# TensorE transpositions as ordinary fp32 matmuls with the identity, in a two-block, one-core transformer kernel

## The chip, the core and the metric

The kernel runs on one core of one Trainium2 chip. The metric is the device time of one execution in microseconds; the median of three runs before the change is 1362.98 us (1362.72 to 1365.19). TensorE (PE) does the matmuls, VectorE (DVE) and ScalarE (ACT) the elementwise work, and GpSimd (POOL) and SyncE (SP) start transfers.

## The reference, cut to what matters

Two blocks of two layers each work on 256 tokens of width 1024, all in fp32. Every layer is a normalisation, a mixer, a residual add, a normalisation and a squared-ReLU MLP:

```python
for layer in range(DEPTH):                      # first block
    u = rms_norm(h, mix_norm_g[layer])
    h = h + even_mixer(u, ...)                  # layer 0: 8 heads of top-k attention, 8 of compressed/selected/window attention
    # layer 1: h = h + diff_mixer(u, ...)       # 8 heads, each the difference of two softmaxes
    h = h + sq_relu_mlp(rms_norm(h, mlp_norm_g[layer]), mlp_w_up[layer], mlp_w_down[layer])
# second block: layer 0 pools over trailing windows, layer 1 is attention of 16 heads with a position bias;
# norms are followed by a scale and shift, residual adds by a gate
```

Transpositions are no part of the mathematics. They are there because a matmul contracts over partitions: the normalised activations, each head's softmax and the attention's output lie with tokens on partitions and are wanted with channels (or keys) on partitions.

## The kernel before

Weights come as a stream of 179 pieces of 1 MB into a ring of four. ACT copies each piece to a rounded form `whi` (L323), DVE makes the remainder `wlo` (L522), and PE forms each product in three passes of the rounded type (helper `three`, L1047). The activations are split likewise into `uh` and `ul`. Almost all of the time is this stream: four MLPs of 32 pieces, three mixers with projections of 10 to 12 pieces in front and 4 behind, and one pooling piece. The order of each engine's work is written out by hand, and semaphores tie the engines together.

PE transposes in these places:

- `norm(e)` (L1105), eight times (e = 0, 1, 2, 3, 5, 6, 7, 8). DVE writes the scaled activations `ut` in quarters (L557), PE turns 16 blocks of 128x128 into four PSUM banks, and after each pair of blocks of the second token half it signals ACT. ACT writes `uh` (L345), or in the second block `work` or `qk` (L349), DVE the rest (L571, or L579 and L580), and the next projection or MLP starts with piece k as soon as `ul` of block k is there.
- `turn` (L1172), once for each head's softmax `P`: 24 heads in layer 0 (phase e), 8 in layer 1 (phase d), 16 in the last attention (phase b). It turns three blocks of 128x128 into bank 3. DVE copies the bank to `PT` (L650), and `values` (L1179 to L1181) multiplies it with the values. PE's order in phases e and b is, per head: scores (L1158) and masks (L1161) of head i, values of head i-3, turn of head i-2. In phase d one turn comes for two scores.
- `turn_out` (L1190), once for each of the three attentions: 16 blocks of the output `o_` into banks 0 to 3, ACT and DVE split them (L385, L655), and `project` (through `add_rows`, L1047) follows.
- two small places (L1259 and L1317), which the change leaves as they are.

`ident` is the fp32 identity in `con`. In layer 0, `hidden` (L1252) is run between the first four heads, and the compressed branch (L1268, L1270, L1280, L1317, L1322) between later ones. DVE and ACT also split four weight pieces between those heads. `spread_col` (L1112) is an ordinary fp32 matmul of a broadcast column with `ident`, 128 columns wide; `swapped` and `dswap` (L1210, L1333) are ordinary fp32 matmuls of 512 columns.

Of the kernel before, what the change touches and what calls it, by code (L numbers as in the profile page):

```python
# [51 lines left out]
TURN = (2, 3, 4, 5)  # L52
# [14 lines left out]
def build(nc, a):  # L67
# [3 lines left out]
    with ctx:  # L71
# [48 lines left out]
        bank = [ctx.enter_context(nc.psum_tensor(f"bank{i}", [128, 512], fp32)) for i in range(8)]  # L120
# [3 lines left out]
        ident = con[:, C_ID:C_ID + 128]  # L124
# [7 lines left out]
        o_ = vo[:, 1, :, :]  # L132
# [4 lines left out]
        ut = uf.rearrange("p (t n) -> p t n", t=NT)  # L137
# [73 lines left out]
        def u_no(e):  # L211

            return 8 * (e if e < 4 else e - 1)
# [20 lines left out]
        def even_map(i):  # L234
            kind, h = i // 8, i % 8
            if kind == 0:
                return QA + h // 2, 64 * (h % 2), KA, tk, slice(0, 64), (4, 5)
            g, j = h // 4, h % 4
            vs = 128 * (kind - 1) + 64 * g
            return QB + j, 64 * g, (KS, KW)[kind - 1], v_, slice(vs, vs + 64), ((6, 7), (4, 5))[kind - 1]  # L240
# [798 lines left out]
        def _(pe):  # L1039
            mm = nc.tensor.matmul  # L1040

            def three(out, w_first, wh, wl, xh, xl, start, stop):

                for i, (wa, xa) in enumerate(((wh, xh), (wh, xl), (wl, xh)) if w_first else
                                             ((wh, xh), (wl, xh), (wh, xl))):
                    st, mv = (wa, xa) if w_first else (xa, wa)
                    ins = mm(out, st, mv, start=start and i == 0, stop=stop and i == 2, skip_group_check=True)  # L1047
                return ins
# [5 lines left out]
            def features(m, out, sems=None, blocks=2):  # L1054

                wh, wl = weights(m)
                for k in range(KB):
                    if sems is not None:
                        s, base, per = sems
                        pe.wait_ge(s, base + k // per + 1)  # L1060
                    for b in range(blocks):
                        c = slice(128 * b, 128 * b + 128)
                        ins = three(out[:, 256 * b:256 * b + 256], True, wh[:, k, c], wl[:, k, c], uh[:, k, :], ul[:, k, :],
                                    k == 0 and b == 0, k == KB - 1)
                return ins

            def tokens(m, out, c0, n, o0=0, width=None, w=None):
                wh, wl = weights(m) if w is None else w
                for t in range(NT):
                    for k in range(KB):  # L1070
                        ts = slice(128 * t, 128 * t + 128)
                        ins = three(out[:, o0 + n * t:o0 + n * t + n], False, wh[:, k, c0:c0 + n], wl[:, k, c0:c0 + n],
                                    uh[:, k, ts], ul[:, k, ts], t == 0 and k == 0 and o0 == 0, k == KB - 1)
                return ins
# [24 lines left out]
            def norm(e):  # L1099
                for t in range(NT):  # L1100
                    for q in range(4):
                        pe.wait_ge(u_ready, u_no(e) + 4 * t + q + 1)
                        for b in (2 * q, 2 * q + 1):
                            c = 256 * (b % 2) + 128 * t
                            ins = nc.tensor.transpose(bank[TURN[q]][:, c:c + 128], ut[:, t, 128 * b:128 * b + 128], ident)  # L1105
                        if t:
                            ins.then_inc(turned, 1)

# [58 lines left out]
            def turn(ph, i, src):  # L1167

                if i >= 1:
                    pe.wait_ge(s_pt[ph], i)  # L1170
                for c in range(3):
                    ins = nc.tensor.transpose(bank[3][:, 128 * c:128 * c + 128], src[:, 128 * c:128 * c + 128], ident)  # L1172
                ins.then_inc(s_tr[ph], 1)

            def values(ph, i, vv, vs, dst):
# [7 lines left out]
            def turn_out(r, after):  # L1183

                pe.wait_ge(o_ready, after)
                for j in range(4):
                    for b in (2 * j, 2 * j + 1):
                        for t in range(NT):
                            c = 256 * (b % 2) + 128 * t
                            ins = nc.tensor.transpose(bank[j][:, c:c + 128], o_[:, t, 128 * b:128 * b + 128], ident)  # L1190
                    ins.then_inc(oT_ready, 1)

            def project(m0, r, e):
# [4 lines left out]

            pe.wait_ge(in_con, 16)
            norm(0)  # L1200

            order = [0, 1, 3, 4, 5, 6, 7, 8, 9]
# [9 lines left out]
            for i in range(10):  # L1212
                pe.wait_ge(lo_ready, i + 1)
                if i == 2:
# [3 lines left out]
                    ins = tokens(i, bank[0], 0, 92, w=w)  # L1218
                elif i in (8, 9):
                    pe.wait_ge(e_t2, order.index(i - 2) + 1)  # L1220
                    features(i, bank[i % 2], blocks=1)
                    ins = tokens(i, bank[i % 2], 128, 128, o0=256)
                else:
# [6 lines left out]
                    ins = features(i, bank[i % 2], (ul_ready, 0, 1) if i == 0 else None)  # L1230
# [56 lines left out]
            for i in range(24 + 3):  # L1287
                if i < 24:
                    q, r0, k, vv, vs, ob = even_map(i)
# [9 lines left out]
                if i >= 3:  # L1299
                    j = i - 3  # L1300
                    q, r0, k, vv, vs, ob = even_map(j)
# [6 lines left out]
                if 2 <= i < 26:  # L1308
                    pe.wait_ge(s_exp["e"], i - 1)
                    turn("e", i - 2, P[:, (i - 2) % 4, :])  # L1310
# [8 lines left out]
                if i == 23:  # L1319
                    pe.wait_ge(o_free, 2)  # L1320
                    for t in range(NT):
                        ins = mm(bank[6 + t][:, :], pcT[0:CW, t, :], vbd[0:CW, :, :], start=True, stop=True)  # L1322
                    ins.then_inc(oc_ps, 1)
            turn_out(0, NT)
            project(MLP0 - 4, 0, 1)
            norm(1)
            mlp(0)
            pe.wait_ge(spread_out, 2)
            norm(2)

            def dswap(i):
# [15 lines left out]
            for i in range(8 + 2):  # L1347
                if i < 8:
                    for c in range(2):
                        scores("d", 2 * i + c, i, 8 + i, 64 * c, causal)  # L1350
                if i >= 2:
                    j = i - 2
                    hs = slice(128 * (j % 4), 128 * (j % 4) + 128)
                    values("d", j, v_, slice(128 * j, 128 * j + 128), [bank[4 + j // 4][:, hs], bank[6 + j // 4][:, hs]])
                if 1 <= i < 9:
                    pe.wait_ge(s_cmb, i)
                    turn("d", i - 1, P[:, 2 * (i - 1) % 4, :])
            turn_out(1, 2 * NT)
            project(MLP1 - 4, 1, 3)
            norm(3)  # L1360
# [8 lines left out]
            for g in range(4):  # L1369
                pe.wait_ge(p_h, g + 1)  # L1370
                for t in range(NT):
                    ts = slice(128 * t, 128 * t + 128)
                    for k in range(2):
                        ins = three(bank[4 + 2 * t + g // 2][:, 256 * (g % 2):256 * (g % 2) + 256], False,
                                    wp[0][:, g, k, :], wp[1][:, g, k, :], uh[:, 2 * g + k, ts], ul[:, 2 * g + k, ts],
                                    g % 2 == 0 and k == 0, g % 2 == 1 and k == 1)
# [21 lines left out]
            for i in range(16 + 3):  # L1398
                if i < 16:
                    pe.wait_ge(h_in[i % 8], 16 * (i // 8 + 1))  # L1400
                    scores("b", i, i // 2, 8 + i // 2, 64 * (i % 2),
                           [(slice(0, 128), flip, hank[:, i % 8, 128:256]), (slice(128, 384), flip, hank[:, i % 8, :])])
                if i >= 3:
                    j = i - 3
                    hs = slice(64 * (j % 8), 64 * (j % 8) + 64)
                    values("b", j, v_, slice(64 * j, 64 * j + 64), [bank[4 + j // 8][:, hs], bank[6 + j // 8][:, hs]])
                if 2 <= i < 18:
                    pe.wait_ge(s_exp["b"], i - 1)
                    turn("b", i - 2, P[:, (i - 2) % 4, :])
            turn_out(2, 3 * NT)  # L1410
            project(MLP3 - 4, 2, 8)
            norm(8)
# [116 lines left out]
```

## Time and profile before

| | |
|---|---|
| median of 3 runs | 1362.98 us |
| the profiled execution's own time | 1365.05 us |
| its span, first to last instruction | 1363.3 us |
| PE busy | 1254.2 us (92%) |
| DVE / ACT busy | 839.5 us (62%) / 546.9 us (40%) |
| mean granted clock of PE | 0.926 |

Between the span and the execution's own time lie 1.75 us. In the trace, a matmul's duration contains a tail in which the next one already runs, so the pace of a run of matmuls is read from their starts, or from a merged row as (its length minus one instruction's length) over (count minus one). The granted clock has two levels here, 1.0 (2.4 GHz) and 0.5 (1.2 GHz). Names such as `bank<-con,P` are the tiles that an instruction writes and reads.

### The profile page before, as it was taken

What the parts mean: (1) busy time and instruction counts of PE and PEld (TensorE: products, weight loads), DVE (VectorE), ACT (ScalarE), POOL (GpSimd) and SP (SyncE); (2) the same over time, 40 slices, a digit from 0 to 9 for tenths busy, and PEclk for the clock granted to TensorE, in tenths of its full rate; (3) what the DMA queues carried; (4) which work ended last, traced back from release to release, by engine and by line L of the source; (5) the groups of instructions that cost most, each with busy time, mean ns of one, the idle gap of its engine ahead of it and who ended that gap; (6) DMA issues with size and microseconds to landing.
All of it is one profiled execution on the core that took longest, in us unless ns stands there. A gap on an engine that the chain in (4) does not pass through costs nothing.

```text
span 1363.3 us, 18272 instructions
## 1 busy us (share of the span) xinstructions
PE 1254.2 (92%) x7662; PEld 1100.6 (81%) x7662; DVE 839.5 (62%) x1168; ACT 546.9 (40%) x754; POOL 44.1 (3%) x86
## 2 busy tenths in 40 slices
PE   5989898899998998699999939999979998899997
PEld 4975676799997986579999838999969877799996
DVE  5662543677777664657777787777773444755554
ACT  5302232544444324344444455444444442544442
POOL 1010000000000000000000000000001010000000
PEclk9998557899999997799999969999989998999999
DMA  8413110587876343057787715777735520455540
GB/s 301 153 47 124 62 62 12 183 290 283 282 281 243 125 155 124 1 201 278 279 280 281 250 64 207 280 281 283 283 138 197 195 72 32 141 183 188 187 150 32
DMA packets 35074, 245.72 MB, mean 180 GB/s; under 512 B 4272, under 2 KB 4304, under 8 KB 6064
## 3 DMA queue, kind: packets, MB, share of 16 engines
q1 hardware_dynamic: 26352, 189.13, 39.3%
q0 software_dynamic: 8496, 54.43, 11.2%
q8 instruction: 61, 1.00, 0.3%
q10 hardware_dynamic: 144, 0.98, 0.2%
q14 instruction: 21, 0.17, 0.0%
HBM read 242.93 MB, written 1.07 MB: 179 GB/s over the span
## 4 chain that ended last, share of the span: by engine, by line
PE 83%; DVE 10%; ACT 4%; issue 2%; DMA 1%; SPq 0%; DVEq 0%; ACTq 0%
PE bank L1047 67%; PE bank L1158 4%; DVE wlo L522 2%; ACT whi L323 2%; PE bank L1172 2%; PE bank L1161 2%; PE bank L1105 1%; PE bank L1252 1%; PE bank L1179 1%; PE bank L1181 1%; PE bank L1180 1%; DMA raw<-in_stream 1%; PE bank L1190 1%; DVE x L538 1%; DVE work L536 1%
## 5 line engine op out<-in xcount | busy, mean ns | idle before, releaser
L522 DVE TENSOR_TENSOR wlo<-raw,whi 128x2048 fp32r<-128x2048 f32 x175 | 399.4, 2283 | 289.8 <-ACT whi L323 289.8
L323 ACT ACTIVATE whi<-raw 128x2048 fp32r<-128x2048 f32 x175 | 333.8, 1909 | 252.9 <-PE bank L1047 251.9
L1047 PE MATMUL bank<-uh,whi 128*128 128x256 f32 x1408 | 406.7, 289 | 4.5 <-DVE ul L571 3.6
L1047 PE MATMUL bank<-ul,whi 128*128 128x256 f32 x1408 | 400.5, 284 | 0.0
L1047 PE MATMUL bank<-uh,wlo 128*128 128x256 f32 x1408 | 400.1, 284 | 0.0
L1047 PEld LDWEIGHTS bank<-uh,whi 128*128 128x128 f32 x1408 | 272.4, 193 | 13.0 <-issue 7.5
L1047 PEld LDWEIGHTS bank<-ul,whi 128*128 128x128 f32 x1408 | 272.4, 193 | 5.1 <-issue 2.9
L1047 PEld LDWEIGHTS bank<-uh,wlo 128*128 128x128 f32 x1408 | 272.1, 193 | 0.0
L1047 PE MATMUL bank<-whi,hh 128*128 128x512 f32 x512 | 200.4, 391 | 2.4 <-DVE hl L597 2.2
L1047 PE MATMUL bank<-wlo,hh 128*128 128x512 f32 x512 | 199.9, 390 | 0.0
L1047 PE MATMUL bank<-whi,hl 128*128 128x512 f32 x512 | 199.2, 389 | 0.0
L359 ACT ACTIVATE work<-bank 128x512 f32<-128x512 f32 x64 | 38.3, 598 | 227.2 <-PE bank L1047 227.2
L1047 PEld LDWEIGHTS bank<-whi,hh 128*128 128x128 f32 x512 | 96.3, 188 | 22.4 <-DVE wlo L522 2.7
L604 DVE CUSTOM_DVE_ANT_0 qk<-qk,cb 128x1024 f32<-128x1024 f32 x96 | 113.4, 1218 | 0.0
L1047 PEld LDWEIGHTS bank<-whi,hl 128*128 128x128 f32 x512 | 96.1, 188 | 20.6
L1047 PEld LDWEIGHTS bank<-wlo,hh 128*128 128x128 f32 x512 | 96.3, 188 | 17.5
L1047 PE MATMUL bank<-whi,uh 128*128 128x512 f32 (+3 forms) x224 | 83.3, 372 | 9.3 <-DVE ul L990 9.3
L377 ACT ACTIVATE P<-bank,nmax 128x128 f32<-128x128 f32 x56 | 20.6, 367 | 154.4 <-DVE nmax L643 154.4
L1047 PE MATMUL bank<-wlo,uh 128*128 128x512 f32 (+3 forms) x224 | 81.5, 364 | 0.0
L1047 PE MATMUL bank<-whi,ul 128*128 128x512 f32 (+3 forms) x224 | 81.3, 363 | 0.0
L1158 PE MATMUL bank<-qk 64*128 64x128 f32 x224 | 68.9, 442 | 5.8 <-ACT P L379 2.1
L1105 PE MATMUL bank<-con,u 128*128 128x128 f32 x128 | 28.0, 407 | 48.8 <-DVE u L557 48.8
(204 smaller groups left out, 1149.2 us busy)
## 6 DMA issues: line engine op xcount, KB each, us to landing
raw<-in_stream SPq DMA_DIRECT2D x178, 1024.0 KB, 4.9
qk<-in_w_mod POOLq DMA_DIRECT2D x48, 1024.0 KB, 5.2
u<-bias_rows POOLq DMA_DIRECT2D x16, 128.0 KB, 4.6
x<-in_x SPq DMA_DIRECT2D x2, 512.0 KB, 8.6
vo<-in_fin_g POOLq DMA_DIRECT2D x2, 512.0 KB, 6.4
out_y<-vo SPq DMA_DIRECT2D x2, 512.0 KB, 2.6
con<-in_con ACTq DMA_DIRECT2D x1, 955.5 KB, 7.4
raw<-in_stream SPq DMA_DIRECT2D x1, 368.0 KB, 14.8
```

The lines of the kernel that those rows point to most:

```text
L323: nc.scalar.activation(whi[:, c % RING, 0:w], raw[:, n % RING, 0:w], ACT.Copy).then_inc(hi_ready, 1)
L359: nc.scalar.activation(work[:, s % 2, :], bank[s % 2][:, :], ACT.Relu).then_inc(relu_done, 1)
L377: nc.scalar.activation(P[:, i % size, 0:128], b[:, 0:128], ACT.Exp, bias=nmax[:, i, 0:1], accum_out=sums[:, i, 0:1])
L522: nc.vector.tensor_tensor(wlo[:, c % RING, 0:w], raw[:, raw_index(c) % RING, 0:w], whi[:, c % RING, 0:w].bitcast(fp32), ALU.subtract).then ...
L536: link(nc.vector.tensor_tensor(work[:, i, :], bank[4 + 2 * t + h][:, :], gate[:, 512 * h:512 * h + 512], ALU.mult))
L538: nc.vector.tensor_tensor(xs, work[:, i, :], xs, ALU.add).then_inc(x_ready, 1)
L604: ins = nc.vector.tensor_tensor_reduce(out=stage[j][:, r, :], in0=stage[j][:, r, :], in1=cb[:, :], scale=1.0, scalar=0.0, op0=ALU.mult, op ...
L1047: ins = mm(out, st, mv, start=start and i == 0, stop=stop and i == 2, skip_group_check=True)
L1105: ins = nc.tensor.transpose(bank[TURN[q]][:, c:c + 128], ut[:, t, 128 * b:128 * b + 128], ident)
L1158: mm(b[:, c0:c1], qk[rows_, q, 128 * t:128 * t + 128], qk[rows_, k, 0:c1 - c0], start=t == 0, stop=False, skip_group_check=True)
L1161: ins = mm(b[:, dst], st, mv, start=False, stop=n == len(masks) - 1, skip_group_check=True)
L1172: ins = nc.tensor.transpose(bank[3][:, 128 * c:128 * c + 128], src[:, 128 * c:128 * c + 128], ident)
```

## The change

Three calls are replaced; operands, destinations, order and semaphores stay:

```diff
@@ norm (L1105) @@
-                            ins = nc.tensor.transpose(bank[TURN[q]][:, c:c + 128], ut[:, t, 128 * b:128 * b + 128], ident)
+                            ins = mm(bank[TURN[q]][:, c:c + 128], ut[:, t, 128 * b:128 * b + 128], ident, start=True, stop=True)
@@ turn (L1172) @@
-                    ins = nc.tensor.transpose(bank[3][:, 128 * c:128 * c + 128], src[:, 128 * c:128 * c + 128], ident)
+                    ins = mm(bank[3][:, 128 * c:128 * c + 128], src[:, 128 * c:128 * c + 128], ident, start=True, stop=True)
@@ turn_out (L1190) @@
-                            ins = nc.tensor.transpose(bank[j][:, c:c + 128], o_[:, t, 128 * b:128 * b + 128], ident)
+                            ins = mm(bank[j][:, c:c + 128], o_[:, t, 128 * b:128 * b + 128], ident, start=True, stop=True)
```

Both forms load the block as the stationary operand and move the identity past it. The old form is PE's transpose mode, the new one a plain fp32 product. The transpositions of L1259 and L1317 keep the old form.

## Rows read from the trace of the kernel before

**Rows 1.** The page: busy time and share of each engine; slices, granted clock.

```profile
PE 1254.2 (92%) x7662; PEld 1100.6 (81%) x7662; DVE 839.5 (62%) x1168; ACT 546.9 (40%) x754; POOL 44.1 (3%) x86
...
PEclk9998557899999997799999969999989998999999
```

**Rows 2.** The page: the chain that ended last, shares of the span by line.

```profile
PE bank L1047 67%; PE bank L1158 4%; DVE wlo L522 2%; ACT whi L323 2%; PE bank L1172 2%; PE bank L1161 2%; PE bank L1105 1%; PE bank L1252 1%; PE bank L1179 1%; PE bank L1181 1%; PE bank L1180 1%; DMA raw<-in_stream 1%; PE bank L1190 1%; DVE x L538 1%; DVE work L536 1%
```

**Rows 3.** Groups by form, TensorE: count | busy, mean ns | idle before.

```profile
L1172 PE MATMUL bank<-con,P 128*128 128x128 f32 x144 | 31.8, 343 | 1.6 <-DVE P L925 1.1 <-ACT P L379 0.4
L1105 PE MATMUL bank<-con,u 128*128 128x128 f32 x128 | 28.0, 407 | 48.8 <-DVE u L557 48.8
...
L1190 PE MATMUL bank<-con,vo 128*128 128x128 f32 x48 | 10.8, 418 | 14.9 <-DVE vo L957 8.4 <-DVE vo L856 3.5 <-DVE vo L1020 3.0
```

**Rows 4.** Timeline, TensorE: start, us, engine, line, operation, form, count (full, full, half, half).

```profile
829.44 1.95 PE L1112 MATMUL bank<-con,mod 128*128 128x128 f32 x16
...
214.27 0.50 PE L1172 MATMUL bank<-con,P 128*128 128x128 f32 x3
...
179.21 0.85 PE L1172 MATMUL bank<-con,P 128*128 128x128 f32 x3
...
251.80 3.68 PE L1105 MATMUL bank<-con,u 128*128 128x128 f32 x16 [3.79 <-DVE u L557]
```

**Rows 5.** The chain in order of time: swaps at half, at full clock.

```profile
39.38 1.76 PE bank L1210 x2
...
466.72 0.86 PE bank L1333 x2
```

**Rows 6.** Stretches: length, busy PE, PEld, DVE, ACT, POOL (instructions), granted clock, DMA.

```profile
571.70:575.00 3.30, 3.19 (x15) 3.19 (x16) 1.27 (x3) 1.71 (x3) 0.00 (x0) 0.50 0.00 0
575.20:578.60 3.40, 3.40 (x17) 2.83 (x16) 1.59 (x3) 0.85 (x2) 0.00 (x0) 1.00 0.00 0
...
164.60:210.40 45.80, 45.72 (x180) 34.27 (x181) 20.88 (x46) 14.57 (x50) 0.00 (x0) 0.50 0.16 60
1094.00:1128.00 34.00, 33.57 (x214) 26.37 (x215) 15.90 (x42) 13.30 (x60) 3.22 (x6) 1.00 0.24 59
...
527.40:544.30 16.90, 14.70 (x54) 9.71 (x53) 10.03 (x31) 7.23 (x33) 0.00 (x0) 0.50 0.18 62
544.50:561.30 16.80, 14.53 (x95) 10.08 (x93) 12.63 (x42) 6.88 (x32) 0.00 (x0) 1.00 0.01 1
```

**Rows 7.** The same for line 1172 alone (turns): PE, PEld, PEclk.

```profile
128.00:213.30 85.30, 16.11 (x57) 12.48 (x57) 0.50 0.14 50
526.00:544.50 18.50, 2.38 (x9) 1.82 (x9) 0.54 0.18 66
```

**Rows 8.** Timeline of layer 0's heads: scores of two in turn, then values.

```profile
176.16 1.65 PE L1158 MATMUL bank<-qk 64*128 64x128 f32 x4
...
179.99 1.65 PE L1158 MATMUL bank<-qk 64*128 64x128 f32 x4
...
181.75 0.64 PE L1179 MATMUL bank<-vo,PT 128*128 128x64 f32 x2
```

**Rows 9.** Timeline: the weight remainder on DVE that covers the turn at 159.47.

```profile
159.51 2.29 DVE L522 TENSOR_TENSOR wlo<-raw,whi 128x2048 fp32r<-128x2048 f32 x1 [2.32 <-ACT whi L323]
```

**Rows 10.** Timeline of norm 1: after its transpositions, and the clock's return.

```profile
255.73 0.55 PE L1047 MATMUL bank<-uh,whi 128*128 128x256 f32 x1 [0.26 <-DVE ul L571]
...
257.79 0.28 PE L1047 MATMUL bank<-uh,whi 128*128 128x256 f32 x1
```

**Rows 11.** Timeline: norm 0's follower, norm 3's transpositions, norm 5's evacuations.

```profile
19.20 0.55 PE L1047 MATMUL bank<-uh,whi 128*128 128x256 f32 x1 [2.29 <-DVE ul L571]
...
599.72 2.48 PE L1105 MATMUL bank<-con,u 128*128 128x128 f32 x16 [2.51 <-DVE u L557]
...
794.33 3.76 ACT L349 ACTIVATE qk<-bank,mod,gain 128x256 f32<-128x256 f32 x8 [2.32 <-PE bank L1105]
```

**Rows 12.** Timeline: the second turn-out.

```profile
571.81 3.61 PE L1190 MATMUL bank<-con,vo 128*128 128x128 f32 x16 [8.44 <-DVE vo L957]
```

## The prediction

> **What bounds the kernel now.** I read first the busy times [rows 1], then the chain that ended last [rows 2]. PE is busy 92% of the span and its lines carry nearly all of the chain, 67% of it in the split products (L1047). So PE is the bound almost everywhere, and what it gets more to do goes into the time unless it waited there anyway. The two largest transposing lines stand in that chain themselves, L1172 with 2% and L1105 with 1%, and L1190 with 1%. The second thing to see is the clock by slices [rows 1]: it is at half in the fifth and sixth slice, which are layer 0's attention, and dips around each normalisation. The stretches say it exactly: twelve heads of layer 0, 164.6 to 210.4, ran at 0.5 with PE busy 45.72 of 45.80 us, while the last attention, 1094 to 1128, ran at 1.0 [rows 6]. The price of the edit must therefore be taken at each of the two levels.
>
> **How many.** 144 turns of a block (48 heads of three), 128 blocks in the eight norms, 48 in the three turn-outs [rows 3]: 320 blocks, all 128x128 fp32. Each is one matmul record now.
>
> **The price of one.** The new form is in the trace already: `spread_col` moves the same identity past a stationary fp32 block of 128 columns. Its 8 products are 16 records in 1.95 us [rows 4]; with about 0.28 for the last one that is (1.95 - 0.28)/15 = 0.111 us a record and 0.223 a product. A transposition at full clock: three in 0.50 us, (0.50 - 0.28)/2 = 0.11 each [rows 4]. So a block costs one record more, 0.113 us at full clock rounded up. At half clock the old form takes (3.68 - 0.42)/15 = 0.217, and three take 0.85 [rows 4]. The new form has no row there at this shape; the nearest is a 512-column product, 1.76 us for two at half against 0.86 at full clock [rows 5], so it doubles, and a block costs 0.213 more at half clock. The bounds: nothing, if the second record hid under the load of its weights (at full clock the sixteen of spread_col show that it doesn't), and 0.45, if the old form were free. I take the row of the same form.
>
> The Trainium skill (TensorE: Matmul & The Clock Gate, Terms) calls the transpose mode four times faster for fp32, and FP8 and Floating Point Precision (TensorE Precision Notes) gives true fp32 four passes. By that the ordinary form would cost four times 0.11; the rows show twice, and the measurement decides.
>
> **Layer 0's turns (24).** 57 records of L1172, 19 turns, lie in 128 to 213.3 at half clock [rows 7]. A head there repeats every 3.83 us (179.99 - 176.16) with PE hardly idle [rows 6, 8]: scores and masks, values from 181.75, the turn behind them. Three blocks add 3 x 0.213 = 0.64, so a head takes 4.47. DVE has 20.88 us of work in those twelve heads, 1.74 each, and covers nothing. One turn, at 159.47, is covered: its copy waits for a weight remainder of 2.29 us on DVE, which ends at 161.8 [rows 9], some 1.5 us after the turn; without that cover it would be another 0.64. 18 x 0.64 = 11.5. The other 5 turns run at full clock, 3 x 0.113 = 0.34 each, on the way to the GELU and at the end: 1.7. Together 13.2.
>
> **Layer 1's turns (8).** Three at half clock [rows 7], 1.9, and five at full, 1.7: 3.6. Here the clock came back by itself within the attention, at about 544.4 [rows 6]. More PE work before that can bring it earlier; the five groups after cost PE less time than those before, and one group earlier is worth about 2.7 us (half of a group of 5.8 us less a wait or two). Between 3.6 and 0.9 I take 2.2.
>
> **The last attention's turns (16).** All at full clock, PE busy 33.57 of 34.00 [rows 6]: 16 x 0.34 = 5.4. The last few wait for copies in a chain with PE, where the price is exposed as well.
>
> **The norms (8).** After five of them (1, 2, 6, 7, 8) the picture is that of norm 1: 16 transpositions at half clock, 0.26 us of waiting, and products at half clock from 255.73, until at about 257.7 the clock is back; a product of 256 columns lasts 0.55 at 255.73 and 0.28 at 257.79 [rows 4, 10]. The old blocks and the products behind them share that half-clock time, and the new blocks take the products' place in it. If the clock comes back at the same moment, the extra work ends up at full clock: 16 x 0.113 = 1.8, less the waiting of 0.26 and a little more where it was longer, so 1.4 each, 7.0 for five. Bounds: 0.5 each (the clock earlier) and 16 x 0.213 = 3.4 (later). Norm 3 ran at full clock, paced by DVE's quarters: 2.48 us for 16 [rows 11]. Sixteen new ones take 16 x 0.223 + 0.1 = 3.7, 1.2 more, but the evacuations that the next product needs are released pair by pair before the last block, so +0.4, bounds 0 and 1.2. Norm 5 feeds the pooling through ACT, 3.76 us for eight evacuations [rows 11], which start after the tenth block and then run beside PE: +0.7, bounds 0.3 and 3.4. Norm 0 is followed by 2.29 us of waiting for the first weights [rows 11], and by products at half clock, 0.55 us for the first: of +3.4 all but about 1 is hidden, and an earlier clock would give about as much back. I take 0, bounds -1 and +1. Sum 8.1.
>
> **The turn-outs (3).** Each is 16 blocks at half clock, 3.6 us [rows 12], with the projection right behind it. By the same reasoning as for the norms 1.8 each less a wait, 4.7 together; bounds 3 and 10.
>
> **What moves besides.** Nothing in order or semaphores. ACT's and DVE's copies start later where PE does, as counted. The ring of weights gains slack in those places. The second weight load per block (0.19) passes beside the matmuls, as for spread_col.
>
> **Sum.** 13.2 + 2.2 + 5.4 + 8.1 + 4.7 = 33.6 us. The profiled execution took 1365.05, with 1363.3 of span and 1.75 around it; 1365.05 + 33.6 = 1398.65. It stood 2.07 above the median of the runs, so the median after is 1396.6, I say 1396.5. The likeliest case's own bounds: 24 (norms and turn-outs at their low ends, layer 1 near 0.5) to about 42 (half of the norms at the high end), 1387 to 1405, with a few us for how the clock falls in layer 0's last heads.
>
> **Rival 1, the clock rises in layer 0's attention (faster).** If ordinary products keep or bring the full clock from 128 us on, PE's work there halves: twelve heads go from 45.8 us to 12 x 4.47/2 = 26.9, and the other 39.5 us of the stretch, mostly PE too, to about 25: 52 in place of 85.3. Then -33 for that stretch in place of +11.5, and the rest, 22.1, remains: -11, 1352. If it comes only for the twelve heads from 164.6 on: 22.1 + 3.8 - 18.9 = +7, 1370. It decides where these heads' work stands to what raised the clock elsewhere. For it: the new blocks are a larger share of the head, and in layer 1 a similar loop came back by itself. Against: transpositions raise the clock as they are. At the second turn-out PE did nothing but transpose from 571.81 to 575, and right then the clock went from 0.50 to 1.00 [rows 6, 12]. So the change doesn't turn a kind of work that counts for nothing into one that counts; it only lengthens a third of each head, and scores of 64 rows and values of 64 columns, which fill the rest at half clock, stay. Layer 1's values are 128 columns wide.
>
> The Trainium skill's rule speaks for this rival: TensorE: Matmul & The Clock Gate, Part 4, has it that the full clock does not engage for transpose mode, since that doesn't count as busy. By it this case would end at 1352. The turn-out's rows contradict it here.
>
> **Rival 2, the price is more than twice (slower still).** If a block cost four times the old one, every item triples, +101, 1464. Against: the sixteen records of spread_col [rows 4].
>
> **Rival 3, the edit does nothing.** The new call could be built into the same instruction, or its second record be hidden: 1363. Against: the two calls' records differ already, 16 records for 8 products against 16 for 16 [rows 4].
>
> **How the numbers follow.** Forecast 0.83; rival 1 in full 0.07, in part 0.05; rival 2 0.03; rival 3 0.02. A measurement of this kernel tells about 0.2%, 2.7 us, from no change. Faster: 0.08; same 0.03; slower 0.89. The range reaches below the likeliest case for layer 1 and the norms coming out cheap together: 1380 to 1405.
>
> **What would show it.** 320 matmul records more, two per block. L1172 at three blocks in about 0.85 at full clock and 1.5 at half; heads of layer 0 every 4.47 us with the clock still at 0.5 from 128 to about 225; heads of the last attention 0.34 longer; each norm's products starting some 2.4 us later but at full clock sooner. It would be wrong, above all, if the clock in layer 0's attention read 1.0.

## The result

The changed kernel takes 1400.01 us (median of 4 executions, 1398.10 to 1400.79), the kernel before on the same chip 1364.09. The ratio is 1.0257, 95% interval 1.0232 to 1.0281: slower by 36 us. The forecast was 1396.5 in 1380 to 1405. The profiled execution took 1400.10 with a span of 1398.3, against 1365.05 and 1363.3. Ratios, here and below, leave out executions more than 1.5% above the fastest of the same kernel, while the medians given with the experiments are of all of them.

The page of the kernel after: busy time and share of each engine, and the granted clock by slices; they answer to [rows 1]. Then the chain that ended last, by line, which answers to [rows 2].

```profile
PE 1296.1 (93%) x7982; PEld 1149.4 (82%) x7982; DVE 840.1 (60%) x1168; ACT 547.1 (39%) x754; POOL 44.2 (3%) x86
...
PEclk9998556999999998899999979999999999999999
...
PE bank L1047 65%; PE bank L1158 4%; PE bank L1172 3%; PE bank L1105 3%; DVE wlo L522 2%; ACT whi L323 2%; PE bank L1161 2%; PE bank L1190 1%; PE bank L1252 1%; PE bank L1179 1%; PE bank L1181 1%; PE bank L1180 1%; DMA raw<-in_stream 1%; DV
```

PE has 7982 records for 7662, the 320 that were foreseen, and is busy 41.9 us longer in a span that is 35.0 longer. The slices (35 us each) show the same picture of the clock: half in layer 0's attention, full nearly everywhere else. In the chain L1172 went from 2% to 3% and L1105 from 1% to 3%. DVE and ACT are busy within 0.6 us of what they were.

The groups by form of the kernel after, TensorE, which answer to [rows 3] (count | busy, mean ns | idle before):

```profile
L1172 PE MATMUL bank<-con,P 128*128 128x128 f32 x288 | 56.4, 347 | 0.7 <-ACT P L379 0.4 <-DVE P L925 0.2
L1105 PE MATMUL bank<-con,u 128*128 128x128 f32 x256 | 48.5, 377 | 48.2 <-DVE u L557 48.2
L1190 PE MATMUL bank<-con,vo 128*128 128x128 f32 x96 | 17.1, 361 | 14.9 <-DVE vo L957 8.4 <-DVE vo L856 3.5 <-DVE vo L1020 3.0
```

Each has twice the records. Busy time rose by 24.6, 20.5 and 6.3 us, together 51.4, and the span by 35.0: PE's busy time as a whole rose by 41.9, so 9.5 of the 51.4 came back in its other lines, where the clock was up sooner; the rest went where PE had waited.

The timeline of two heads of layer 0 and of one of the last attention, kernel after (start, us, engine, line, operation, form, count). They answer to the half-clock turn of [rows 4] and to [rows 8]:

```profile
187.43 1.59 PE L1172 MATMUL bank<-con,P 128*128 128x128 f32 x6
...
192.00 1.59 PE L1172 MATMUL bank<-con,P 128*128 128x128 f32 x6
...
1138.27 0.89 PE L1172 MATMUL bank<-con,P 128*128 128x128 f32 x6
...
1141.31 0.89 PE L1172 MATMUL bank<-con,P 128*128 128x128 f32 x6
```

A head of layer 0 repeats every 4.57 us, where it was 3.83, and one of the last attention every 3.04, where it was 2.65: a full-clock turn went from 0.50 to 0.89.

Stretches of the kernel after (length, busy PE, PEld, DVE, ACT, POOL with instructions, granted clock, DMA share, GB/s): layer 0 at half clock, the two parts of layer 1, and part of norm 3's transpositions. The second and third answer to the last two of [rows 6].

```profile
128.90:224.40 95.50, 93.51 (x375) 74.87 (x374) 39.93 (x98) 23.94 (x77) 0.00 (x0) 0.50 0.13 45
541.90:555.50 13.60, 12.45 (x46) 8.13 (x45) 8.48 (x22) 6.70 (x26) 0.00 (x0) 0.50 0.25 84
555.70:576.00 20.30, 19.47 (x134) 14.65 (x133) 15.02 (x50) 8.60 (x40) 0.00 (x0) 1.00 0.00 1
617.00:620.40 3.40, 3.40 (x19) 3.40 (x18) 1.06 (x4) 0.52 (x2) 0.00 (x0) 0.51 0.99 336
```

Layer 0 stays at half clock for 95.5 us (85.3 before), so the first rival did not occur. Layer 1 is at half clock for 13.6 us where it was 16.9. Norm 3, which ran at full clock before [rows 11], has a stretch at half.

The timelines of norms 1, 2, 3 and 8, kernel after: the transpositions, and the product that follows them. Norm 1 answers to the last line of [rows 4] and to [rows 10], norm 3 to [rows 11].

```profile
264.98 5.47 PE L1105 MATMUL bank<-con,u 128*128 128x128 f32 x32 [3.79 <-DVE u L557]
270.65 0.36 PE L1047 MATMUL bank<-uh,whi 128*128 128x256 f32 x1 [0.20 <-DVE ul L571]
...
457.99 6.42 PE L1105 MATMUL bank<-con,u 128*128 128x128 f32 x32 [4.56 <-DVE u L557]
464.17 0.36 PE L1047 MATMUL bank<-uh,whi 128*128 128x256 f32 x1
...
616.08 5.47 PE L1105 MATMUL bank<-con,u 128*128 128x128 f32 x32 [2.51 <-DVE u L557]
621.38 0.36 PE L1047 MATMUL bank<-uh,whi 128*128 128x256 f32 x1
...
1201.90 6.53 PE L1105 MATMUL bank<-con,u 128*128 128x128 f32 x32 [5.23 <-DVE u L557]
1208.18 0.36 PE L1047 MATMUL bank<-uh,whi 128*128 128x256 f32 x1
```

The same of norms 2 and 8 in the kernel before:

```profile
444.00 3.65 PE L1105 MATMUL bank<-con,u 128*128 128x128 f32 x16 [4.57 <-DVE u L557]
447.91 0.55 PE L1047 MATMUL bank<-uh,whi 128*128 128x256 f32 x1 [0.26 <-DVE ul L571]
...
1169.19 3.59 PE L1105 MATMUL bank<-con,u 128*128 128x128 f32 x16 [5.23 <-DVE u L557]
1173.17 0.36 PE L1047 MATMUL bank<-uh,whi 128*128 128x256 f32 x1 [0.40 <-DVE ul L580]
```

These products now start at full clock (0.36 us). In norms 1 and 2 they had started at half (0.55): the clock now comes back inside the longer transpositions, which is the exchange the forecast counted on. Norm 8's product stood at 0.36 before, so there was little to exchange. The size differs from norm to norm.

### Where the time went

The table cuts the traces at instructions of DVE that all of them have, and gives how many us longer each step became (the sums are of unrounded steps). The three parts of the change were then run alone (next section), so their columns stand beside. Each column is one trace against one trace of the kernel before, whose own executions range from 1362 to 1368 us in most groups; so a step of a microsecond counts only where several columns agree.

| step | forecast | whole change | turns alone | norms alone | turn-outs alone | old form twice |
|---|---|---|---|---|---|---|
| up to norm 0 | 0 | -1.3 | -0.5 | -1.3 | 0.0 | -0.5 |
| norm 0 | 0 | 1.1 | 0.0 | 1.0 | 0.0 | 0.0 |
| up to the first attention | 0 | -1.4 | -1.0 | -1.6 | -1.2 | 1.6 |
| layer 0's attention | 13.2 | 13.1 | 15.7 | -0.6 | -0.8 | 12.0 |
| turn-out 1 | 1.6 | 1.7 | -0.2 | -0.1 | 1.7 | -0.7 |
| norms 1 and 2 | 2.8 | 2.7 | -0.2 | 2.7 | -1.8 | -0.5 |
| layer 1's attention | 2.2 | -1.4 | -0.8 | 6.8 | 8.6 | -1.0 |
| turn-out 2 | 1.6 | 1.9 | 0.3 | 0.3 | 2.5 | 0.4 |
| norm 3 | 0.4 | 2.1 | 0.7 | 2.3 | 0.8 | 0.7 |
| norm 5 | 0.7 | 2.2 | 0.0 | 1.6 | 0.0 | 0.0 |
| norms 6 and 7 | 2.8 | 4.1 | -0.2 | 3.5 | -0.6 | -0.1 |
| last attention | 5.4 | 5.9 | 5.9 | 0.4 | 0.6 | 6.4 |
| turn-out 3 | 1.6 | 2.0 | 0.1 | 1.3 | 2.6 | 0.1 |
| norm 8 | 1.4 | 2.3 | 0.0 | 2.2 | 0.8 | 0.0 |
| sum | 33.6 | 35.0 | 19.9 | 18.7 | 13.2 | 18.4 |

### The profile page after: what moved, and what is told of

It is laid out like the page before. It is cut to its first block, busy times and chain, and to the rows that moved or that the text cites. A ratio compares the mean times of both kernels' runs of the same rounds, so it can differ in the third digit from the quotient of the medians.

```text
span 1398.3 us, 18912 instructions
## 1 busy us (share of the span) xinstructions
PE 1296.1 (93%) x7982; PEld 1149.4 (82%) x7982; DVE 840.1 (60%) x1168; ACT 547.1 (39%) x754; POOL 44.2 (3%) x86
## 4 chain that ended last, share of the span: by engine, by line
PE 84%; DVE 9%; ACT 4%; issue 2%; DMA 1%; SPq 0%; DVEq 0%; ACTq 0%
PE bank L1047 65%; PE bank L1158 4%; PE bank L1172 3%; PE bank L1105 3%; DVE wlo L522 2%; ACT whi L323 2%; PE bank L1161 2%; PE bank L1190 1%; PE bank L1252 1%; PE bank L1179 1%; PE bank L1181 1%; PE bank L1180 1%; DMA raw<-in_stream 1%; DVE x L538 1%; DVE work L536 1%
## 5 line engine op out<-in xcount | busy, mean ns | idle before, releaser
L1047 PEld LDWEIGHTS bank<-whi,hl 128*128 128x128 f32 x512 | 96.1, 188 | 20.5
L1105 PE MATMUL bank<-con,u 128*128 128x128 f32 x256 | 48.5, 377 | 48.2 <-DVE u L557 48.2
L1105 PEld LDWEIGHTS bank<-con,u 128*128 128x128 f32 x256 | 47.0, 288 | 50.6 <-issue 31.5
```

What stands on the lines that cost most here:

```text
L1105: ins = mm(bank[TURN[q]][:, c:c + 128], ut[:, t, 128 * b:128 * b + 128], ident, start=True, stop=True)
```

## The experiments

The theory after the result: each block costs its second record at the clock of its place, and the clock reacts to how long PE works without a wait, whichever form it executes. The rival: transpositions don't count for the clock and plain products do, so part of the price was paid back in clock. A second question is what sets layer 1's clock, since that step went against its forecast.

### The three parts alone

The turns alone (L1172 only):

```
-                    ins = nc.tensor.transpose(bank[3][:, 128 * c:128 * c + 128], ...
+                    ins = mm(bank[3][:, 128 * c:128 * c + 128], ..., start=True, stop=True)
```

> Only line 1172, the 48 turns of three blocks, in the new form. Theory (PE pays one record more per block, at the clock of the place): layer 0 +13, the last attention +5.9, layer 1 between -1.4 and +3.6 according to when the clock comes back there, so +18 to +22 us over the kernel before, ratio 1.013 to 1.016. Rival (the turns brought only the parts that add up in the trace, and the norms' larger steps came from the turns' shift of the clock): more than +24.

The norms alone have the same edit at L1105 only:

> Only line 1105, the 8 norms, in the new form. By the step table of the changed kernel each norm gives 0.8 to 2.3 us and the start gives back 1 to 2.6: +11 to +14 us. By the prediction's terms: +8. If the larger steps of norms 3 and 5 came from where the clock's low stretch happened to lie in that execution, the sum lies between.

The turn-outs alone have it at L1190 only:

> Only line 1190, the 3 turn-outs, in the new form: +5 to +6 us (steps of 1.7, 1.9 and 2.0 in the changed kernel; the prediction had 4.7).

Measured: turns 1383.98 us, ratio 1.0140 (1.0108 to 1.0172); norms 1384.26, 1.0137 (1.0115 to 1.0159); turn-outs 1379.10, 1.0104 (1.0080 to 1.0129). The turns are 17.1 us over the kernel before by the medians and 19.9 by the spans, for +18 to +22. In the steps that each part touches the three agree with the whole change within 1 us, but for layer 0's attention, 15.7 against 13.1. But their spans add up to 51.7 us where the whole change took 35.0. Of the 16.7 us between, some 16 lie in layer 1's attention alone, where turn-outs and norms touch nothing. Stretches there, first of the kernel with the turn-outs alone:

```profile
527.00:545.00 18.00, 16.92 (x59) 11.17 (x60) 10.37 (x36) 7.09 (x32) 0.00 (x0) 0.50 0.16 58
545.00:565.90 20.90, 20.90 (x78) 14.46 (x76) 9.35 (x30) 7.30 (x32) 0.00 (x0) 0.50 0.00 1
```

With the norms alone:

```profile
531.50:562.30 30.80, 29.92 (x108) 20.57 (x108) 16.00 (x52) 10.85 (x48) 0.00 (x0) 0.50 0.05 19
```

And with the turns alone:

```profile
541.00:554.60 13.60, 11.52 (x43) 7.98 (x42) 8.04 (x24) 5.53 (x25) 0.00 (x0) 0.50 0.21 78
```

Where the turns of layer 1 are short, its attention could stay at half clock to its end, although PE was busy 20.90 of 20.90 us there; where they are long, the clock came back after 13.6 us. That is why the parts don't add up. It also means that a part costed alone by its measured total would be charged with 7 to 9 us that are not its own. The turn-outs (12.2 us by the medians, for +5 to +6) and the norms (17.3, for +11 to +14) missed their expectations by that. It was not one odd execution: the lowest of four lies 15.7 and 20.4 us above the lowest of the kernel before (1378.13 and 1382.90 against 1362.48), where the steps without layer 1's attention add up to 4.5 and 11.9. Why an edit elsewhere keeps layer 1's clock down is not shown.

### The old form, twice

This kernel keeps the transpose mode and turns every block of L1172 twice, the second time onto the same place:

```
                 for c in range(3):
+                    for _ in range(2):
                         ins = nc.tensor.transpose(bank[3][:, 128 * c:128 * c + 128], ...
```

> Line 1172 keeps transpose mode, but every block is transposed twice into the same place (the second is superfluous), so that PE has as many records as with plain products. Theory (only the records' time counts, and the clock treats both forms alike): within 3 us of x1_turns, layer 0 at the half clock from 128 us on in both, layer 1's clock coming back as early as in x1_turns. Rival (transpose mode doesn't count as activity for the clock): layer 1's clock comes back later than in x1_turns or not at all, 3 us and more on top of x1_turns.

Measured: 1381.94 us, ratio 1.0121 (1.0099 to 1.0144), beside 1.0140 for the plain products. A turn of layer 0 in it, timeline (the loop shifts the line to L1173), and its stretches in layer 1:

```profile
186.64 1.49 PE L1173 MATMUL bank<-con,P 128*128 128x128 f32 x6
...
538.90:552.60 13.70, 11.75 (x45) 7.80 (x44) 8.24 (x24) 5.74 (x25) 0.00 (x0) 0.51 0.22 78
552.80:556.20 3.40, 3.40 (x25) 2.46 (x24) 2.32 (x8) 1.82 (x8) 0.00 (x0) 1.00 0.00 0
```

Six transpositions take 1.49 us and six records of plain products 1.59: the ordinary form costs twice the old one and 0.1 us for each turn besides. Half clock ends in layer 1 after 13.7 us, as with plain products (13.6). So the clock came back for transpositions as it did for products, and the time is 15.0 us over the kernel before by the medians, where the plain products' is 17.1. The rival falls.

The Trainium skill (TensorE: Matmul & The Clock Gate, Part 4) says that the full clock doesn't engage for transpose mode, which doesn't count as busy in the same way. The two stretches just shown disagree, and so does the next experiment.

### PE's waits in layer 0 filled, by either form

Before the scores' and values' products that wait, superfluous transpositions of a constant go to an unused part of a bank: 20 while PE waits for the GELU, 12 between the compressed scores, 28 at the compressed probabilities. The second kernel does the same with half as many plain products.

```
+            def fill(n, out):
+                for _ in range(2 * n):
+                    nc.tensor.transpose(out[:, 384:512], swap, ident)
```

> The kernel before, with transpositions (transpose mode, superfluous, into unused columns of bank 6) in three places of layer 0's attention where PE waits or has hardly any columns to pass: 20 of them before the transposition of the GELU's result, 12 between the compressed scores, 20 and twice 4 around the transposition of the compressed probabilities. Theory (transpose mode keeps the clock up like any product): the clock stays at 1.0 past 128 us, at least until a later wait, and heads of layer 0 take about 2.1 us instead of 3.83; 10 to 30 us faster. Rival (transpose mode doesn't count for the clock): half clock from 128 us on as before, 2 to 5 us slower.

> The same places filled with plain fp32 products of 128 columns, half as many, so that PE is filled for the same time. Both theories: the clock stays at 1.0 past 128 us and the time falls; the theory expects the same clock stretches as with transpositions within one or two us of the places, the rival expects only this one to gain.

Measured (one execution each, so no ratio): 1368.21 and 1373.29 us, beside 1362.61 for the kernel before. The expected gain in time, 10 to 30 us, did not come; the clock in layer 0 did. Timeline of the first, filled with transpositions:

```profile
157.29 3.48 PE L1045 MATMUL bank<-con 128*128 128x128 f32 x20
...
162.04 0.92 PE L1163 MATMUL bank<-qk 64*128 64x128 f32 x4
...
163.69 0.50 PE L1177 MATMUL bank<-con,P 128*128 128x128 f32 x3
164.12 0.92 PE L1163 MATMUL bank<-qk 64*128 64x128 f32 x4
...
174.11 0.69 PE L1184 MATMUL bank<-vo,PT 128*128 128x64 f32 x2 [2.44 <-DVE PT L650]
```

The clock stayed full to 135.5 (128 before), was half to 159.4, rose in the middle of 20 transpositions and held to 173.1: scores take 0.92 for 1.65, and a head 2.08 us (162.04 to 164.12) for 3.83. It fell again around a wait of 2.44 us for DVE. Filled with plain products the clock went the same way: full to 140.5, half to 164.4, full to 178.0. That is 5 us later each time, and 4.2 of it is the later start of this kernel's first attention. Stretches of this second kernel:

```profile
140.70:164.40 23.70, 23.70 (x99) 19.21 (x98) 11.79 (x36) 5.55 (x18) 0.00 (x0) 0.50 0.12 39
164.60:178.00 13.40, 11.59 (x83) 8.63 (x81) 8.07 (x17) 4.54 (x13) 0.00 (x0) 1.00 0.18 72
```

Layer 0's attention got 5.3 and 5.9 us shorter, and layer 1's 6.7 and 10.0 longer, at half clock from end to end again (524.7 to 555.5 in the first). What was gained was lost there.

### Filling wherever PE waits

If the waits let the clock fall, filling them all should hold it. The filling is superfluous work again: plain products of 512 columns before the norms, the turn-outs and at the start, of 128 columns in layer 0.

```
+            def keep(n, out):
+                for _ in range(n):
+                    mm(out[:, :], ident, con[:, C_COS:C_COS + 512], start=True, stop=True)
...
+                keep({0: 3, 1: 8, 2: 10, 3: 5, 5: 16, 6: 12, 7: 15, 8: 11}[e], bank[0])
...
+                keep((8, 19, 9)[r], bank[0])
```

> The kernel before (transpose mode kept), with superfluous plain fp32 products into unused PSUM wherever PE waits for DVE or ACT for more than about 2 us: ahead of each norm and turn-out, ahead of the first attention, at its GELU, compressed scores, compressed probabilities and two weight remainders, and at the start of layer 1's attention. Theory (the waits are what takes the clock down, and anything PE streams keeps it up): layer 0's heads at 2.1 us for nearly all 24, the norms' transpositions at full clock; 35 to 65 us faster, 1300 to 1330. Rival (the clock in layer 0 falls for what its heads are, rather than for the waits): half clock again within the heads, less than 15 us faster.

The same with the change under study in it:

> k1_keep with the change on top (all three places in plain products). Theory: one record more per block at the full clock, 320 x 0.113 = 36, less what hides in norms paced by DVE (about 7), plus 0.05 for the entry of each turn: +28 to +36 us over k1_keep. Rival (the price depends on low clock for most of its size): under +20.

Measured: 1395.76 us (1388.09 to 1402.19), ratio 1.0254 (1.0224 to 1.0283); with the change 1413.13, 1.0374 (1.0355 to 1.0393). The change on top cost 17.4 us by the medians and 24.8 by the profiled spans, both under the +28 to +36 that was expected; the medians lie in the rival's range (under +20) and the first kernel's executions spread over 14 us, so this pair does not price the change. The first forecast, 1300 to 1330, was wrong by 66 us at its upper end. The mean clock did rise, to 0.979 (0.926 before), and layer 0's attention became 14.0 us shorter. The timeline of the first, ahead of norm 5, shows the mistake:

```profile
782.77 17.01 PE L1045 MATMUL bank<-con 128*128 128x512 f32 x32 [3.94 <-ACT vo L392]
799.62 0.60 PE L1116 MATMUL bank<-con,u 128*128 128x128 f32 x4
```

Sixteen products of 512 columns are 32 records, which I had counted as 16: the filling is twice as long as the wait and delays the norm, by 12.6 us in this place alone. A filling of half the size follows. Besides what is shown, it has three products for seven ahead of the first attention, two for four in layer 1's, and none between the compressed scores:

```
-                keep({0: 3, 1: 8, 2: 10, 3: 5, 5: 16, 6: 12, 7: 15, 8: 11}[e], bank[0])
+                keep({0: 0, 1: 4, 2: 5, 3: 2, 5: 8, 6: 6, 7: 7, 8: 5}[e], bank[0])
...
-                keep((8, 19, 9)[r], bank[0])
+                keep((4, 9, 3)[r], bank[0])
```

> k1_keep with its filling cut to the waits: a filling product of 512 columns is 0.86 us at full clock and not 0.43 as sized for k1_keep, so their numbers are halved, and none stand between the compressed scores (those products take 0.14 us a record at either clock). Theory: PE's waits keep their length and the clock stays up in nearly all of them; 1315 to 1340, 25 to 45 us faster than the kernel before. Rival (the filling delays the work behind it as much as the clock gives back): within 10 us of the kernel before.

> k3_keep_fit with the change on top. At the full clock a block costs 0.113 us more, 320 blocks 36, less about 7 under DVE's pace in the norms and 5 for the half-clock stretch in layer 0 being longer or shorter: +22 to +34 over k3_keep_fit. k1_keep and k2_keep_plain, with oversized filling, lay 24.8 us apart by their spans.

Measured: 1342.12 us, ratio 0.9810 (0.9752 to 0.9868), so this one, with superfluous products in it and the old form of transposition, beats both kernels in three of its four executions (1336.52 to 1343.72); the fourth took 1364.32, with a mean clock of 0.952 for 0.970 to 0.976, so the filling does not always hold the clock. With the change: 1364.63 (ten executions, 1350.88 to 1366.85 and one of 1404.91), 0.9970 (0.9932 to 1.0008), 22.5 us more, at the low end of the +22 to +34 expected. One execution of the kernel before in this group, of thirteen, took 3042.46 us, and is not in the ratios. Stretches of the fitted kernel: layer 0 before and after its clock comes back, and layer 1.

```profile
135.50:152.30 16.80, 16.80 (x69) 13.21 (x70) 10.82 (x34) 4.83 (x14) 0.00 (x0) 0.50 0.15 59
152.50:220.00 67.50, 64.88 (x387) 50.25 (x387) 38.52 (x70) 24.05 (x62) 0.00 (x0) 1.00 0.23 79
500.60:531.30 30.70, 29.97 (x108) 20.56 (x108) 15.87 (x51) 10.86 (x48) 0.00 (x0) 0.50 0.04 18
```

Layer 0's attention is 24.0 us shorter than before. The wait that had brought the clock down at 173 in the kernel with fillings in layer 0 alone is covered. The timeline there:

```profile
164.33 2.45 PE L1050 MATMUL bank<-con 128*128 128x128 f32 x20
166.94 0.43 PE L1190 MATMUL bank<-vo,PT 128*128 128x64 f32 x2 [0.15 <-DVE PT L650]
```

Twenty records end 0.15 us before the values can start, and the clock stays. This pair also gives the change's price where the clock is nearly always full. Norm 2, timeline, without the change:

```profile
414.34 2.48 PE L1116 MATMUL bank<-con,u 128*128 128x128 f32 x16 [0.19 <-DVE u L557]
417.57 0.35 PE L1057 MATMUL bank<-uh,whi 128*128 128x256 f32 x1 [0.75 <-DVE ul L571]
```

And with it:

```profile
425.26 3.84 PE L1116 MATMUL bank<-con,u 128*128 128x128 f32 x32 [0.19 <-DVE u L557]
429.30 0.36 PE L1057 MATMUL bank<-uh,whi 128*128 128x256 f32 x1 [0.20 <-DVE ul L571]
```

From the first transposition to the first product it is 3.23 us without and 4.04 with: the transpositions take 1.36 longer, 0.55 of it in the place of a wait for DVE. The price of a norm at full clock is 0.8 us, six times over in this pair (norms 1 to 3 and 6 to 8, and 1.35 for norm 5, 1.2 for norm 0). Against the kernel before, without fillings, the change cost up to 2.3.

### Layer 1's clock by itself

The kernel before, in which only the eight turns of layer 1 transpose twice:

```
                 for c in range(3):
+                    for _ in range(2 if ph == "d" else 1):
                         ins = nc.tensor.transpose(bank[3][:, 128 * c:128 * c + 128], ...
```

> The kernel before, in which only the eight turns of layer 1 transpose each of their three blocks twice (the second time onto the same place, so the output is the same); everything else is as before. Theory (longer turns bring layer 1's clock back one group earlier, and transpositions do it as well as plain products): half clock in layer 1 ends about 3 us earlier, layer 1's attention ends 1 to 2 us sooner than in the kernel before although PE gets 24 transpositions more, and over several runs the time is 1 to 3 us below the median of before or equal to it, ratio 0.998 to 1.000. Rival (layer 1's clock is chance and the turns have no part in it): the 24 extra blocks cost their own time, 9 blocks at 0.21 and 15 at 0.11, 3.6 us, and the ratio is 1.0026.

And the fitted filling with that edit, and with norm 5's filling halved:

> The last filling kernel (superfluous plain products in PE's waits, old transpose form) with two edits: layer 1's turns transpose each block twice, as in the kernel beside this, and the filling ahead of norm 5 is halved (4 products of 512 columns for 8). Theory: layer 1's attention, at half clock throughout in that kernel's profile (500.6 to 531.3), gets its clock back after some 13 us, worth 5 to 8 us, and norm 5's overlong filling gives back 3 to 4 us: 1330 to 1336 us where the filling kernel took 1342, ratio to before 0.974 to 0.980. Rival (the clock in layer 1 doesn't depend on its turns): only norm 5's gain, less 3 us for the blocks, about 1341.

Measured: 1363.54 us, median of 12, ratio 0.9990 (0.9978 to 1.0001). Twenty-four superfluous transpositions cost nothing that can be told, and the 1.0026 of their own price is excluded. Stretches of this kernel in layer 1:

```profile
524.20:537.80 13.60, 11.50 (x43) 7.77 (x42) 8.12 (x25) 5.53 (x25) 0.00 (x0) 0.50 0.21 77
538.00:558.00 20.00, 18.89 (x130) 13.75 (x128) 14.50 (x49) 8.70 (x40) 0.00 (x0) 1.00 0.00 1
```

Half clock lasts 13.6 us for the 16.9 of [rows 6], and the step is 1.0 us shorter. So layer 1's -1.4 in the whole change needs nothing but its longer turns. In this trace the gain does not last: from the start of turn-out 2 to norm 5 the kernel lost 1.1 us again against the kernel before.

The fitted filling with it had an execution profiled at 1332.95 us, ratio 0.9772 (0.9747 to 0.9797). Its layer 1, a stretch that was at half clock in the fitted kernel:

```profile
500.90:527.90 27.00, 25.40 (x170) 18.15 (x168) 19.69 (x67) 13.20 (x62) 0.00 (x0) 1.00 0.09 37
```

Of its six executions three took 1333 to 1337 us and three 1354 to 1360, and the ratio rests on the first three; the median of all six is 1345.51. That it is faster than the fitted filling is therefore not shown.

## Why the prediction was right, and where its terms were off

**The bound and the count held.** PE's time goes into the span: 320 records more, no other engine's work changed, and L1172 and L1105 grew in the chain (L1190 stayed at 1%).

**The price of one block held.** Twice the old form, 0.213 us more at half clock: six transpositions in 1.49 against three in 0.85 give (1.49 - 0.85)/3 = 0.213, exact. But plain products cost 0.10 more for each turn (1.59 against 1.49), and at full clock a turn costs 0.39 more in place of 0.34. I had taken the price of a record from inside a run of sixteen, where such an entry can't be seen. Twenty-four turns at 0.1 and less come to some 2 us in layer 0, 0.8 in the last attention.

The Trainium skill (TensorE: Matmul & The Clock Gate, Terms) has the transpose mode four times faster for fp32. Here three blocks take 0.50 us where the ordinary form takes 0.89, and 0.85 where it takes 1.59: just under twice, as the second rival's rejection had it, and the measurement decides.

**Layer 0's turns: 13.1 for 13.2**, with two errors that cancel. A head became 0.75 longer and not 0.64, which over 18 turns is 2 us more. Against it the clock fell later in the work: PE came out of a wait at 127.0 and still ran its values at full clock until 128.9, and from one copy of DVE (124.4 in the kernel before) to the next (130.6) the whole change lost 0.67 us of its delay where the turns alone gained 0.85. That is 1.5 us of luck. Before the first turn the step had another 0.5 gained. With the turns alone the step cost 15.7, but 0.8 of it arose before the first turn, where half clock lasted from 93.9 to 104.2 (97.4 to 104.2 before). The 14.9 that remain are near the sum without luck: 18 x 0.75 + 5 x 0.39 = 15.4.

**Layer 1's turns: -1.4 for 2.2.** The step of the working that failed is "between 3.6 and 0.9 I take 2.2". The mechanism was named (the clock can come back a group earlier) but taken at a middle weight. All four kernels with long turns and no filling (whole change, turns alone, old form twice, layer 1 alone) show it, between -0.8 and -1.4: in these traces it was the rule, not a half chance, and it brought more than the blocks cost. It lies below the forecast's own low bound for layer 1, near 0.5.

**The last attention: 5.9 for 5.4.** 16 x 0.387 = 6.2 by the heads of the timeline; the entry cost is the difference.

**The norms: 14.5 for 8.1**, the largest miss. The mis-sized term is "if the clock comes back at the same moment". In norm 1 it came back before the transpositions ended, and the price was 0.8, near the low bound. In norm 2 the stretch at half ended 5.4 us after the first transposition, where before it ended after 4.8: 1.8. In norm 8 before, half clock ended at 1172.5, and after it lasts to 1207.5: 3.3 and 5.6 us after the first transposition, so more of the new blocks were paid at 0.21: 2.3. The forecast had also read norm 8 as norm 1, with half-clock products behind it; they were at full clock already (0.36), so nothing was there to exchange.

Norm 7 shows a path that the forecast left out. Its products ended 1.45 us later, as forecast, but the step cost 2.2: DVE's splits and what follows them start when the transpositions end, whatever the products' clock, and PE then waited 1.08 us for DVE (`gain`, L627) where it had waited 0.29.

Norm 3 is an error of kind: I took "ran at full clock" for a property of the place, 0.4, but after the same wait of 2.51 us the clock now fell in its transpositions, which took 3.0 us longer and not 1.2; it cost 2.1. The turns alone, which leave norm 3 in the old form, have half clock there too (612.7 to 616.2) and pay 0.7 for it, so a third of this is a shift of the clock and not the price of the blocks.

Norm 5 was taken for hidden by ACT's evacuations (0.7). ACT had waited 2.32 us for PE, now it waits 4.55:

```profile
815.02 3.30 ACT L349 ACTIVATE qk<-bank,mod,gain 128x256 f32<-128x256 f32 x7 [4.55 <-PE bank L1105]
```

That line is of the kernel after, timeline, and the one before stands in [rows 11]; the 2.23 more of waiting are the whole cost of the norm, 2.2. In norm 0, taken at 0, 1.1 was not hidden, inside its bounds.

**The turn-outs: 5.6 for 4.7.** 1.7, 1.9 and 2.0 each for 1.6: right in kind, a little late in the clock.

**Start of the kernel: -2.7, not forecast, and luck.** Inputs landed 1.3 us earlier, and the first attention started another 1.4 sooner. Neither has to do with the change: the first is between -1.3 and 0 in the experiments, and the second between -1.2 and +1.6 in the three that edit nothing ahead of it (turns alone, turn-outs alone, old form twice).

**The sum.** -0.1 (layer 0), -3.6 (layer 1), +0.5 (last attention), +6.4 (norms), +0.9 (turn-outs), -2.7 (start) make +1.4, and so 35.0 for 33.6. The mechanism and the price of a block were right. That the sum came this close was luck: the norms were too low by as much as layer 1 was too high and the start, which no term covered, gave back, and in layer 0 two errors cancelled. The range did not foresee this pairing either. Its upper end, 42, stood for half of the norms dear, its lower ones for norms and layer 1 cheap together; norms dear with layer 1 below its bound fell in the middle. (A slip without effect: twelve heads of 4.47 us at twice the speed are 26.8 us, not 26.9, in the first rival.)

**The rivals.** The first, clock up in layer 0, is refuted by the 95.5 us at 0.50, and its reason by the old form twice. That the clock can be raised there is true, but what does it is a filled wait, in either form. The second is refuted by 1.59 for six records, the third by 7982 records.

What stays open: what decides in a single execution whether layer 1 gets its clock back, where PE is busy 20.90 of 20.90 us and yet stays at half. In the traces with longer turns it came back after 13.7 us at the latest. With short turns it took 16.9 us in the kernel before and 30.7 and more, to the end of the attention, with the norms alone, the turn-outs alone, layer 0 filled and the fitted filling; only the oversized filling kept it throughout. So the length of PE's work without a wait, the theory after the result, does not explain it alone.

## What to carry to other kernels

Transpose fp32 blocks in PE's transpose mode: the plain product with the identity is two records for one, 0.11 us a block at full clock and 0.21 at half, and 0.05 (full) to 0.1 (half) more for each turn of three, and it buys nothing in clock. Read off PE's waits before the stretches at half clock: superfluous work that fits such a wait kept the clock in most executions and took 1.9% off this kernel in three of four, and about twice that filling, longer than the waits, cost 2.5%. An edit in a kernel whose clock moves can cost or bring 7 to 9 us in a stage that it doesn't touch, so compare stage by stage before adding up parts.

## What the runs showed of the hardware

- Transpositions raise the granted clock: from 0.50 to 1.00 in the middle of 20 of them, behind ordinary work, and at the kernel before's second turn-out [rows 6, 12] with nothing else from 571.81 us on.
- Six plain-product records take 1.59 us at half clock behind products of 64 columns, where six transpositions take 1.49. That the second weight load isn't covered there is an argument, not shown.
- PE busy without a gap does not by itself bring the clock back: 20.90 of 20.90 us at 0.50 in layer 1 with the turn-outs alone. The products there are scores of 64 rows, among others.
